# Five sixths of the modulation's matrix product computed by VectorE and ScalarE in place of TensorE

## The chip, the core and the metric

The kernel runs on one core of a Trainium2 chip. The metric is the device time of one execution in microseconds (us). TensorE (PE) multiplies matrices; loading its weights is a separate row (PEld). VectorE (DVE), ScalarE (ACT) and GpSimd (POOL) do the rest; SyncE (SP) issues nearly all DMAs, in order, from one queue.

## The reference

Two transformer blocks run one after the other. The first has two layers over 256 tokens and, in layer 0, 256 context tokens, 1024 features each. What the change touches is each layer's modulation:

```python
silu_c = jax.nn.silu(c)                 # (1, 1024)
silu_cc = jax.nn.silu(c_ctx)            # (1024,)
for layer in range(DEPTH):              # DEPTH = 2
    mod = (silu_c @ w_mod[layer] + b_mod[layer])[:, None, :]
    mod_c = silu_cc @ w_mod[layer] + b_mod[layer]
    shift1, scale1, gate1, shift2, scale2, gate2 = jnp.split(mod, N_MOD, axis=-1)
    c_shift1, c_scale1, c_gate1, c_shift2, c_scale2, c_gate2 = jnp.split(mod_c, N_MOD, axis=-1)
    h_ctx = modulate(rms_norm(ctx, norm_mix[layer]), c_shift1, c_scale1)
    h = modulate(rms_norm(x, norm_mix[layer]), shift1, scale1)
    ...
    x = x + gate1 * x_mix
    x = x + gate2 * swiglu(modulate(rms_norm(x, norm_ffn[layer]), shift2, scale2),
                           w_gate_up[layer], w_down[layer])
```

`w_mod[layer]` is 1024 x 6144: 48 blocks of 128 output features, two vectors (`c`, `c_ctx`) to multiply. Around it stand the head projections, a gated long convolution ("hyena") with a small filter network, attention, a merge of both branches with sigmoid gates, and a SwiGLU. The second block (attention, memory attention, 32 experts) is not touched.

## The kernel before

Activations lie with 128 features on the partitions; a product is over all 512 tokens in layer 0 and over 256 in layer 1. Every engine runs a program written out by hand, and semaphores (`Signal`) order them.

**The weight stream.** All weights come as units of 128 x 1024 values, 512 KB, through a ring of six slots (`NS = 6`). `stream_order` (line 237) fixes the order; unit i takes slot i mod 6, and `sync_program` issues it once the user of unit i - 6 is done (`stream.spent`). The queue is in order: a unit that has to wait holds up all behind it.

**Split weights.** For nearly all weights a product is taken in three parts of a reduced type. ScalarE rounds a unit into one of three buffers (`ac_split`, line 416; `NHI = 3`), VectorE subtracts that from the unit in place (`ve_split`, line 426), and TensorE multiplies (`pe_block`, line 435): 24 matmuls a unit. The split of a unit waits until TensorE has finished the unit three before it. Steps ask for `unit + 2`, counted in the stream's order.

**The modulation.** `pe_mod_group` (line 539) multiplies four units (a group of 4 x 128 output features) by the two conditions, 8 matmuls of 512 columns; ScalarE copies the rows out (`ac_mod_group`), and TensorE turns them onto the partitions (`pe_mod_turn`, 4 small matmuls). `ve_mod_finish` adds the bias. Each layer has 12 groups. Of layer 0, groups 0 to 4 run at the start and 5 to 11 in the first seven steps of the hyena stage; of layer 1, group 0 runs ahead of layer 0's gate/up stage, 1 to 10 in its steps 1 to 10, and 11 ahead of layer 1. `pe_prepare`, `ac_prepare` and `ve_prepare` put the groups and the filter network's steps together.

**The stages of a layer**: heads, hyena (12 products), attention with the convolution, merge (`pe_merge`: per step j two gate products, one of `w_o_attn`, and four plain matmuls of `w_o_hyena`, of which one unit serves two steps), `w_out` (`pe_mix_out`, 8 products), gate/up (`pe_gate_up`: 22 steps of two units), down (`pe_down`: two halves of 11 units). In the merge, ScalarE's and VectorE's programs for step j first make splits and then the sigmoids and multiplies of the step.

Of the kernel before, what the change touches and what calls it, by code (L numbers as in the profile page):

```python
# [232 lines left out]
STREAM = [("w_mod", 48), ("w_in", 40), ("w_o_attn", 8), ("w_o_hyena", 4), ("w_out", 8), ("w_gate_up", 44), ("w_down", 22)]  # L233
STREAM2 = [("w_xk_2", 8), ("w_in_2", 22), ("w_out_2", 8), ("w_xq_2", 8), ("w_xv_2", 8), ("w_xo_2", 8)]


def stream_order():
    units = []
    for l in range(2):
        for name, n in STREAM:  # L240
            if name == "w_mod":
                units += [(name, l, u) for u in (range(20) if l == 0 else range(44, 48))]
            elif name == "w_in":
                for u in range(24):
                    units.append((name, l, u))
                    if l == 0 and 12 <= u < 19:
                        units += [("w_mod", 0, 4 * u - 28 + m) for m in range(4)]
                for j in range(8):
                    units += [("w_in", l, 24 + 2 * j), ("w_in", l, 25 + 2 * j), ("w_o_attn", l, j)]
                    if j % 2 == 0:  # L250
                        units.append(("w_o_hyena", l, j // 2))
            elif name == "w_gate_up":
                units += [("w_mod", 1, u) for u in range(4 if l == 0 else 0)]
                for u in range(n):
                    units.append((name, l, u))
                    if l == 0 and u % 2 == 1 and 3 <= u <= 21:
                        units += [("w_mod", 1, 2 * u - 2 + m) for m in range(4)]
            elif name not in ("w_o_attn", "w_o_hyena"):
                units += [(name, l, u) for u in range(n)]
    for name, n in STREAM2:  # L260
        units += [(name, 0, u) for u in range(n)]
    return units
# [10 lines left out]
def two_blocks_kernel(nc, T):  # L273
    ctx = ExitStack()
    with ctx:
# [38 lines left out]
        rst = [sb(f"rst{i}", 512) for i in range(2)]  # L314
        PP = [sb(f"PP{i}", 512) for i in range(2)]
# [66 lines left out]
        landed = {n: (sem("d_" + n), 16) for n in ("vec", "x", "con", "fil0", "fw0", "fil1", "fw1", "mem", "wr", "br", "late",  # L382
# [74 lines left out]
        def unit(name, l, b):  # L457
            return where[name, l, b // UB]

# [79 lines left out]
        def pe_mod_group(pe, l, g):  # L539
            if g == 0:  # L540
                banks.hold((ve_mod, ("added", l, 1)), "mods", l)
            out = banks.take((ac_mod, ("rows", l, g)), "mod", l, g)
            pe.wait_ge(*banks.emptied("mod", l, g))
            pe.wait_ge(*ve_mod.at("silu", 1))
            for k in range(8):
                w, u = stream.block("w_mod", l, 32 * g + 4 * k, 4)
# [4 lines left out]
                stream.spent[u] = (pe_mod, ("group", l, g))  # L551
            ins.then_inc(*pe_mod.up("group", l, g))
            if g > 0 and g != 4:
                pe_mod_turn(pe, l, g - 1)
            if g == 3:
                pe_mod_turn(pe, l, g)

        def pe_mod_turn(pe, l, g):
            if g == 0:
                pe.wait_ge(*banks.emptied("mods", l))  # L560
                pe.wait_ge(*landed["con"])
            if g == 4:
                pe.wait_ge(*ve_mod.at("added", l, 0))
            pe.wait_ge(*ac_mod.at("rows", l, g))
            for n in range(4):
                j = 4 * g + n
                ins = pe.eng.matmul(banks.ap("mods", l)[:, 2 * j:2 * j + 2], rmod[g % 2][:, n * P:(n + 1) * P], cc("sel", 0, 2),
                                    start=True, stop=True)
            ins.then_inc(*pe_mod.up("turn", l, g))
            if g == 11:  # L570
                banks.give("mods", l)

        def ac_mod_group(ac, l, g):
            for u in range(4):
                ac_split(ac, where["w_mod", l, 4 * g + u] + 2)
            ac.wait_ge(*pe_mod.at("group", l, g))
            if g >= 2:
                ac.wait_ge(*pe_mod.at("turn", l, g - 2))
            ac.eng.activation(rmod[g % 2][:, :], banks.ap("mod", l, g), ACT.Copy).then_inc(*ac_mod.up("rows", l, g))

        def ve_mod_group(ve, l, g):
            for u in range(4):
                ve_split(ve, where["w_mod", l, 4 * g + u] + 2)
            if g == 3:
                ve_mod_finish(ve, l, 0)

        def ve_mod_finish(ve, l, part):
            j0, j1 = ((0, 16), (16, 48))[part]
            md, at = MODS[l], 8 + 24 * part
            ve.wait_ge(*pe_mod.at("turn", l, (3, 11)[part]))  # L590
            ve.wait_ge(*landed["vec"])
            ve.eng.tensor_tensor(md[:, j0:j1, :], banks.ap("mods", l)[:, 2 * j0:2 * j1].rearrange("p (j s) -> p j s", s=2),
                                 vv(("b_mod", l), j0, j1 - j0).unsqueeze(2).to_broadcast([P, j1 - j0, 2]),
                                 ALU.add).then_inc(*ve_mod.up("added", l, part))
            ve.wait_ge(*ve_mod.last())
            for s in range(2):
                ve.eng.scalar_tensor_tensor(A12S[l][:, part, :, s], md[:, at:at + 8, s], 1.0,
# [1762 lines left out]
```

## Time and profile before

| | us |
|---|---|
| median of three runs | 2406.33 |
| lowest, highest | 2399.57, 2409.31 |
| the profiled execution's own time | 2409.14 |
| its span in the profile | 2407.4 |

The profiler's page gives each engine's busy time, the queues, the chain of work that ended last and the costliest groups of instructions. Behind it, the trace can be asked for the chain in order of time (each piece with its start, its length and what it was), for a timeline of one engine (each row: start, length, engine, line, operation, output<-inputs; in brackets the engine's idle time before it and what ended that), and for the busy times in a stretch. L12 is line 12 of the kernel. SPq is SyncE's queue. Busy times of different engines overlap.

### The profile page before, as it was taken

How to read it: one execution, taken by the hardware profiler on the slowest of the kernel's cores; microseconds unless marked ns; L12 is line 12 of the kernel's file. 1: busy time of each engine (PE TensorE's matmuls, PEld its weight loads, DVE VectorE, ACT ScalarE, POOL GpSimd, SP SyncE). 2: the span in 40 equal slices, each digit the busy share in tenths (PEclk: the TensorE clock that was granted, in tenths of full speed). 3: DMA queues.
4: the chain of work that ended last, by engine and by line, in shares of the span. 5: the costliest groups of instructions: out<-in, count | busy, mean ns of one | idle time of the engine just before them, and what ended most of it. 6: DMA issues, size and time to landing. Idle time of an engine off the chain costs nothing.

```text
span 2407.4 us, 34019 instructions
## 1 busy us (share of the span) xinstructions
PE 2143.4 (89%) x14596; PEld 1636.3 (68%) x14596; DVE 1032.3 (43%) x1691; ACT 714.3 (30%) x1177; POOL 15.4 (1%) x31
## 2 busy tenths in 40 slices
PE   6989989997999999978998999986689898888886
PEld 2756667775777877668698999885488754445442
DVE  3663663334332334468655566685643311101111
ACT  3222333223322233343444445432533200000000
POOL 0000000000000000000000000000000000000000
PEclk9989999998999999988999999998799899999998
DMA  7226102132454222223145455441042799999993
GB/s 305 71 96 245 44 1 88 62 139 87 175 210 175 97 95 89 96 81 113 36 149 184 158 173 169 150 135 67 14 136 70 291 421 420 420 420 420 420 420 152
DMA packets 90495, 426.93 MB, mean 177 GB/s; under 512 B 10851, under 2 KB 12388, under 8 KB 65380
## 3 DMA queue, kind: packets, MB, share of 16 engines
q1 hardware_dynamic: 89908, 420.96, 46.2%
q10 hardware_dynamic: 432, 3.74, 0.4%
q8 instruction: 117, 1.92, 0.3%
q14 instruction: 38, 0.31, 0.0%
HBM read 423.61 MB, written 1.05 MB: 176 GB/s over the span
## 4 chain that ended last, share of the span: by engine, by line
PE 68%; DMA 12%; DVE 12%; ACT 4%; issue 3%; SPq 1%; POOL 0%; DVEq 0%; ACTq 0%; POOLq 0%
PE bank L452 42%; PE bank L1290 7%; DMA area<-in_w 6%; PE bank L1894 4%; DMA ring<-in_w 4%; PE bank L470 3%; DVE ring_r L431 2%; PE bank L1860 2%; DVE rst L500 2%; PE bank L1002 1%; PE bank L977 1%; PE bank L549 1%; ACT his_r L423 1%; DMA ring<-in_w_mod 1%; SPq L2219 1%
## 5 line engine op out<-in xcount | busy, mean ns | idle before, releaser
L452 PE MATMUL bank<-HH_r,his_r 128*128 128x256 f32 (+1 forms) x1696 | 579.9, 342 | 67.5 <-DVE ring_r L431 50.5
L452 PE MATMUL bank<-HH_r,ring_r 128*128 128x256 f32 (+1 forms) x1696 | 560.1, 330 | 0.0
L431 DVE TENSOR_TENSOR ring_r<-ring,his_r 128x1024 fp32r<-128x1024 f32 x306 | 373.1, 1224 | 412.7 <-ACT his_r L423 412.1
L452 PE MATMUL bank<-H_r,his_r 128*128 128x256 f32 (+1 forms) x1504 | 505.1, 336 | 0.0
L423 ACT ACTIVATE his_r<-ring 128x1024 fp32r<-128x1024 f32 x306 | 322.2, 1056 | 568.3 <-PE bank L452 332.2
L452 PEld LDWEIGHTS bank<-HH_r,his_r 128*128 128x128 f32 x1696 | 328.5, 194 | 111.5 <-issue 67.7
L452 PEld LDWEIGHTS bank<-HH_r,ring_r 128*128 128x128 f32 x1696 | 327.5, 193 | 29.6
L452 PEld LDWEIGHTS bank<-H_r,his_r 128*128 128x128 f32 x1504 | 292.0, 194 | 31.2 <-issue 2.6
L1876 DVE TENSOR_TENSOR tmp<-tmp,bank 128x128 f32<-128x128 f32 x64 | 18.4, 288 | 371.3 <-ACT tmp L1869 290.8
L1290 PE MATMUL bank<-VT_r,his_r 128*128 128x512 f32 (+1 forms) x352 | 120.4, 342 | 8.3 <-DVE YF_r L1103 7.8
L452 PE MATMUL bank<-area_r,his_r 128*128 128x256 f32 (+1 forms) x384 | 122.4, 319 | 0.0
L1894 PE MATMUL bank<-area,tmp 128*32 128x512 f32 x248 | 111.5, 594 | 10.7 <-DVE tmp L1915 6.7
L1290 PE MATMUL bank<-VT_r,ring_r 128*128 128x512 f32 (+1 forms) x352 | 118.4, 336 | 0.0
L1290 PE MATMUL bank<-YF_r,his_r 128*128 128x512 f32 (+1 forms) x352 | 118.4, 336 | 0.0
L470 PE MATMUL bank<-tmp,ones 128*128 128x256 f32 (+1 forms) x220 | 85.3, 494 | 32.1 <-ACT tmp L478 12.3
L1860 PE MATMUL bank<-area,KF 128*32 128x128 f32 x2144 | 89.3, 284 | 15.8 <-DMA area<-in_w 15.3
L500 DVE RECIPROCAL rst<-rst 128x256 f32<-128x256 f32 (+1 forms) x33 | 81.7, 2477 | 43.1 <-ACT rst L494 43.1
L1869 ACT ACTIVATE tmp<-bank 128x128 f32<-128x128 f32 x32 | 8.9, 278 | 299.9 <-PE bank L1860 299.9
L1860 PEld LDWEIGHTS bank<-area,KF 128*32 128x32 f32 x2144 | 72.3, 113 | 28.7 <-DMA area<-in_w 19.4
L1894 PEld LDWEIGHTS bank<-area,tmp 128*32 128x32 f32 x248 | 25.6, 110 | 85.8 <-issue 65.7
L1290 PEld LDWEIGHTS bank<-VT_r,his_r 128*128 128x128 f32 x352 | 66.4, 189 | 18.6 <-issue 4.7
L470 PEld LDWEIGHTS bank<-tmp,ones 128*128 128x128 f32 x220 | 37.7, 201 | 59.4 <-ACT tmp L478 28.8
(306 smaller groups left out, 3001.2 us busy)
## 6 DMA issues: line engine op xcount, KB each, us to landing
area<-in_w SPq DMA_DIRECT2D x98, 1024.0 KB, 27.0
ring<-in_w_in SPq DMA_DIRECT2D x102, 512.0 KB, 3.5
ring<-in_w_mod SPq DMA_DIRECT2D x96, 512.0 KB, 5.3
ring<-in_w_gate_up SPq DMA_DIRECT2D x88, 512.0 KB, 3.5
ring<-in_w SPq DMA_DIRECT2D x39, 1024.0 KB, 26.9
HH<-in_w SPq DMA_DIRECT2D x28, 1024.0 KB, 26.5
ring<-in_w_down SPq DMA_DIRECT2D x44, 512.0 KB, 3.5
con<-in_w SPq DMA_DIRECT2D x14, 1024.0 KB, 25.4
```

The source lines that it names most:

```text
L423: ac.eng.activation(hi_slot(n), stream.slot(u), ACT.Copy).then_inc(*ac_hi.up(n))
L431: ve.eng.tensor_tensor(lo_slot(u), stream.slot(u), hi_slot(n).bitcast(F32), ALU.subtract).then_inc(*ve_lo.up(n))
L452: ins = pe.eng.matmul(out, a, b, start=k == 0 and m == 0, stop=end)
L470: pe.eng.matmul(banks.ap("sum", site)[:, 0:cols], ones[:, :], s[:, 0:cols], start=n == 0, stop=n == total - 1).then_inc(*pe_sums.up(site, n))
L500: ve.eng.reciprocal(r, r).then_inc(*ve_norm.up("rstd", site))
L549: ins = pe.eng.matmul(out[32 * c:32 * c + 32, :], sc2[:, k, :], w, start=k < 4, stop=k >= 4, tile_position=(0, 32 * c))
L977: ins = pe.eng.matmul(out[:, 256 * m:256 * m + c.nkey], q[:, qb * P:(qb + 1) * P], k, start=x == 0, stop=x == len(pairs) - 1)
L1002: ins = pe.eng.matmul(out[:, 0:256], vs(kc), c.pts[g % 2][:, kc * 256:(kc + 1) * 256], start=kc == 0, stop=kc == c.nk - 1)
L1290: ins = pe.eng.matmul(out[n][:, 0:t], w, x, start=k == 0 and m == 0, stop=k == 21 and m == 2)
L1860: ins = pe.eng.matmul(out[32 * n:32 * n + 32, 0:P], HG[g % 2][:, k, 32 * j:32 * j + 32], w, start=k == 0, stop=k == 7, tile_position=(0, 3 ...
L1894: ins = pe.eng.matmul(out[32 * j:32 * j + 32, :], AT[i][:, 32 * k:32 * k + 32], w, start=k == 0, stop=k == 3, tile_position=(0, 32 * j))
L2219: sp.eng.dma_start(experts.slot(i), T[name][e, u]).then_inc(experts.arrived(i)[0], 16)
```

## The change

Only the first 16 of layer 0's 48 blocks stay on TensorE (groups 0 to 3, at the start). The other 80 blocks, 32 of layer 0 and 48 of layer 1, are each one new unit of the stream, `w_mod_rows`: 128 output features on the partitions, 1024 inputs in a row. For each, called a column below, VectorE multiplies the unit by silu(c), broadcast over the partitions, into one buffer (`rsts_flat`), and by silu(c_ctx) in place; ScalarE runs a copy over each product whose accumulator gives the row's sum, straight into `MODS`. The broadcast vectors are loaded and made in the merge stage of layer 0 (`ac_conditions`, `ac_silu`, `ve_silu`), in the attention's buffers `PT` and `PP`.

In the stream a column stands behind each weight unit of layer 0's merge (steps 1 to 7, not behind `w_o_hyena`), the first three `w_out` units, all 44 gate/up units and the first 12 down units. Splits now ask for two split units on (`two_on`), not two stream units on. The filter network's steps stay where they were; `pe_prepare` and its fellows become `pe_filter_step`.

```diff
+MOD_ORDER = [(0, j) for j in range(16, 48)] + [(1, j) for j in range(48)]
 def stream_order():
-    units = []
+    mods = iter([("w_mod_rows", l, j) for l, j in MOD_ORDER])
+    units = [("w_mod", 0, u) for u in range(16)]
     for l in range(2):
...
+        def also(wanted):
+            return [u for u in (next(mods, None) for _ in range(1 if wanted else 0)) if u]
+
+        units += [("w_in", l, u) for u in range(24)]
+        for j in range(8):
+            for name, u in (("w_in", 24 + 2 * j), ("w_in", 25 + 2 * j), ("w_o_attn", j)):
+                units += [(name, l, u)] + also(l == 0 and j)
+            if j % 2 == 0:
+                units.append(("w_o_hyena", l, j // 2))
+        for u in range(8):
+            units += [("w_out", l, u)] + also(l == 0 and u < 3)
+        for name, n in (("w_gate_up", 44), ("w_down", 22)):
+            for u in range(n):
+                units += [(name, l, u)] + also(l == 0)
...
+        def two_on(i):
+            return cut_units[min(nth[i] + 2, len(cut_units) - 1)] if i in nth else i + 2
...
+        COND = [PT[:, :], PPS[:, :]]
+
+        def ac_conditions(ac):
+            ac.wait_ge(*pe_turned.at("ctx0", 7, 0))
+            ac.wait_ge(*pe_values.at("ctx0", 7, 0))
+            for s in range(2):
+                ac.eng.dma_start(COND[s], T["conditions"][s:s + 1, :].to_broadcast([P, 1024])).then_inc(*landed[f"cond{s}"])
+
+        def ac_silu(ac):
+            for s in range(2):
+                ac.wait_ge(*landed[f"cond{s}"])
+                if s:
+                    ac.wait_ge(*ve_mod.at("condition", 0))
+                ac.eng.activation(rsts_flat[:, :], COND[s], ACT.Sigmoid).then_inc(*ac_mod.up("sigmoid", s))
+
+        def ve_mod_column(ve, n):
+            l, j = MOD_ORDER[n]
+            u = where["w_mod_rows", l, j]
+            w = stream.slot(u)
+            ve.wait_ge(*stream.arrived(u))
+            if n:
+                ve.wait_ge(*ac_mod.at("sum", n - 1, 0))
+            else:
+                ve.wait_ge(*ve_mod.at("condition", 1))
+            ve.eng.tensor_tensor(rsts_flat[:, :], w, COND[0], ALU.mult).then_inc(*ve_mod.up("product", n, 0))
+            ve.eng.tensor_tensor(w, w, COND[1], ALU.mult).then_inc(*ve_mod.up("product", n, 1))
+
+        def ac_mod_column(ac, n):
+            l, j = MOD_ORDER[n]
+            u = where["w_mod_rows", l, j]
+            for s, prod in enumerate((rsts_flat[:, :], stream.slot(u))):
+                ac.wait_ge(*ve_mod.at("product", n, s))
+                ac.eng.activation(prod, prod, ACT.Copy, accum_out=MODS[l][:, j, s:s + 1]).then_inc(*ac_mod.up("sum", n, s))
+            stream.spent[u] = (ac_mod, ("sum", n, 1))
...
         def hyena_steps(l, j):
-            return [5 + j] if l == 0 and j < 8 else [12] if l == 1 and j == 0 else []
+            return [5 + j] if l == 0 else []
...
             for j in range(8):
                 for u in merge_units(l, j):
-                    ac_split(ac, u + 2)
+                    ac_split(ac, two_on(u))
+                    ac_mod_after(ac, *stream.units[u])
+                if l == 0 and j == 0:
+                    ac_silu(ac)
                 ac.wait_ge(*(ve_out.at("merged", l, j - 1) if j else ve_cut.at("att", l, 7)))
...
             for j in range(22):
-                ac_split(ac, unit("w_gate_up", l, 16 * j) + 2)
-                ac_split(ac, unit("w_gate_up", l, 16 * j + 8) + 2)
+                for s in range(2):
+                    ac_split(ac, two_on(unit("w_gate_up", l, 16 * j + 8 * s)))
+                    ac_mod_after(ac, "w_gate_up", l, 2 * j + s)
                 ac.wait_ge(*pe_products.at("gate", l, j))
                 ac.eng.activation(AFF[:, j, 0:t], banks.ap("gate", l, j)[:, 0:t], ACT.Sigmoid).then_inc(*ac_out.up("gate", l, j))
-                if l == 0 and 1 <= j <= 10:
-                    ac_prepare(ac, 1, j)
+                if l == 0:
+                    ac_filter_step(ac, 1, j)
...
-                    ac_split(ac, unit("w_down", l, 88 * half + 4 * k) + 2)
+                    ac_split(ac, two_on(unit("w_down", l, 88 * half + 4 * k)))
+                    if k % 2 == 0:
+                        ac_mod_after(ac, "w_down", l, 11 * half + k // 2)
...
-    arrays["w_mod"] = fours(I["w_mod"])
+    arrays["w_mod"] = fours(I["w_mod"][0:1, :, 0:2048])
+    arrays["w_mod_rows"] = np.ascontiguousarray(I["w_mod"].transpose(0, 2, 1)).reshape(2, 48, P, 1024)
+    arrays["conditions"] = np.concatenate([I["c"].reshape(1, 1024), I["c_ctx"].reshape(1, 1024)], axis=0)
```

VectorE's programs change in the same places, with `ve_mod_after` behind each `ve_split`. The bias is added in pieces (`ve_mod_columns_done`), each ahead of its first use.

How the order moves, first on SP's queue in layer 0's merge. `in_w_in` are the gate weights, two a step; `pe_products` is TensorE's signal that a product is done, `ac_mod` ScalarE's that a column is summed. Before, from `w_o_attn` of step 1 to the gate weights of step 4:

```order
L2200 DMA ring<-in_w_o_attn 128x1024 [waits pe_products]
L2200 DMA ring<-in_w_in 128x1024 [waits pe_products] x2
L2200 DMA ring<-in_w_o_attn 128x1024 [waits pe_products]
L2200 DMA ring<-in_w_o_hyena 128x1024
L2200 DMA ring<-in_w_in 128x1024 x2
L2200 DMA ring<-in_w_o_attn 128x1024 [waits pe_products]
L2200 DMA ring<-in_w_in 128x1024 [waits pe_products] x2
```

Now, from the second gate weight of step 2 to the first of step 4:

```order
L2270 DMA ring<-in_w_in 128x1024
L2270 DMA ring<-in_w_mod_rows 128x1024 [waits ac_mod]
L2270 DMA ring<-in_w_o_attn 128x1024
L2270 DMA ring<-in_w_mod_rows 128x1024 [waits ac_mod]
L2270 DMA ring<-in_w_o_hyena 128x1024 [waits pe_products]
L2270 DMA ring<-in_w_in 128x1024 [waits ac_mod]
L2270 DMA ring<-in_w_mod_rows 128x1024 [waits pe_products]
L2270 DMA ring<-in_w_in 128x1024 [waits ac_mod]
L2270 DMA ring<-in_w_mod_rows 128x1024 [waits pe_products]
L2270 DMA ring<-in_w_o_attn 128x1024 [waits ac_mod]
L2270 DMA ring<-in_w_mod_rows 128x1024 [waits pe_products]
L2270 DMA ring<-in_w_in 128x1024
```

A column stands behind each weight. In step 2 the columns wait for ScalarE and the weights for TensorE; behind `w_o_hyena` it is the other way round, and the last column shown takes the slot of `w_o_hyena` itself.

On ScalarE in layer 0's gate/up, two steps before (L423 is the split, L1240 the gate's sigmoid):

```order
L423 ACTIVATE his_r<-ring 128x1024 [waits pe_products,s_w2]
L423 ACTIVATE his_r<-ring 128x1024 [waits pe_products,s_w3]
L1240 ACTIVATE area<-bank 128x512
L423 ACTIVATE his_r<-ring 128x1024 [waits pe_products,s_w4]
L423 ACTIVATE his_r<-ring 128x1024 [waits pe_products,s_w5]
L1240 ACTIVATE area<-bank 128x512
```

and one step now (L422 the split, L643 the two sums of a column, L1305 the sigmoid):

```order
L422 ACTIVATE his_r<-ring 128x1024 [waits pe_products,s_w4]
L643 ACTIVATE rst,MOD<-rst 128x1024 [waits ve_mod]
L643 ACTIVATE ring,MOD<-ring 128x1024 [waits ve_mod]
L422 ACTIVATE his_r<-ring 128x1024 [waits pe_products,s_w0]
L643 ACTIVATE rst,MOD<-rst 128x1024 [waits ve_mod]
L643 ACTIVATE ring,MOD<-ring 128x1024 [waits ve_mod]
L1305 ACTIVATE area<-bank 128x512
```

Two sums, which wait for VectorE, now stand between one split and the next. VectorE in the same step before:

```order
L431 TENSOR_TENSOR ring_r<-ring,his_r 128x1024 [waits ac_hi,s_w4]
L431 TENSOR_TENSOR ring_r<-ring,his_r 128x1024 [waits ac_hi,s_w5]
L1257 TENSOR_TENSOR area<-area,bank 128x512 [waits ac_out]
L1260 TENSOR_TENSOR area<-area,bank 128x512 [waits pe_products,ve_out]
L431 TENSOR_TENSOR ring_r<-ring,his_r 128x1024 [waits ac_hi,s_w0]
```

and now (L430 the split's subtraction, L635 and L636 the column's multiplies, L1323 and L1326 the gating):

```order
L430 TENSOR_TENSOR ring_r<-ring,his_r 128x1024 [waits ac_hi,s_w2]
L635 TENSOR_TENSOR rst<-ring,PT 128x1024 [waits ac_mod,s_w5]
L636 TENSOR_TENSOR ring<-ring,PP 128x1024
L430 TENSOR_TENSOR ring_r<-ring,his_r 128x1024 [waits ac_hi,s_w4]
L635 TENSOR_TENSOR rst<-ring,PT 128x1024 [waits ac_mod,s_w1]
L636 TENSOR_TENSOR ring<-ring,PP 128x1024
L1323 TENSOR_TENSOR area<-area,bank 128x512 [waits ac_out]
L1326 TENSOR_TENSOR area<-area,bank 128x512 [waits pe_products,ve_out]
```

Each subtraction waits for ScalarE's split, and each pair of multiplies stands behind it.

## Rows read from the trace of the kernel before

**Rows 1.** The page, section 1: busy us, share of the span, instructions.
```profile
PE 2143.4 (89%) x14596; PEld 1636.3 (68%) x14596; DVE 1032.3 (43%) x1691; ACT 714.3 (30%) x1177; POOL 15.4 (1%) x31
```
**Rows 2.** Windows, gate/up of layer 0: us; PE, PEld, DVE, ACT, POOL; clock; DMA.
```profile
593.00:883.60 290.60, 285.64 (x1315) 216.66 (x1315) 98.06 (x124) 78.90 (x96) 0.62 (x1) 0.98 0.43 152
```
**Rows 3.** Chain of waits, hyena stage of layer 0: start, length, what.
```profile
159.93 6.11 PE bank L452 x21
...
169.68 5.75 PE bank L452 x24
...
178.27 3.63 PE bank L647 x8
...
199.79 3.54 PE bank L672 x8
...
223.97 8.20 DMA ring<-in_w_in
...
234.63 7.15 PE bank L452 x24
...
242.57 22.11 PE bank L452 x96
```
**Rows 4.** Chain of waits, gate/up of layer 0.
```profile
643.17 3.46 DMA ring<-in_w_gate_up
...
677.04 1.85 PE bank L549 x16
678.89 0.98 PE bank L567 x8
```
**Rows 5.** Chain of waits, hyena stage of layer 1.
```profile
1118.99 0.79 PE bank L567 x8
```
**Rows 6.** Timeline of VectorE, gate/up of layer 0.
```profile
596.23 1.23 DVE L431 TENSOR_TENSOR ring_r<-ring,his_r 128x1024 fp32r<-128x1024 f32 x1
...
619.82 1.22 DVE L431 TENSOR_TENSOR ring_r<-ring,his_r 128x1024 fp32r<-128x1024 f32 x1 [3.97 <-ACT his_r L423]
620.96 0.53 DVE L633 TENSOR_SCALAR YF<-bank,vec 64x256 f32<-64x256 f32 x1
...
623.07 0.29 DVE L615 TENSOR_SCALAR YF<-YF 64x256 f32<-64x256 f32 x1
```
**Rows 7.** Timeline of ScalarE, gate/up of layer 0.
```profile
623.39 0.42 ACT L639 ACTIVATE YF<-YF 64x256 f32<-64x256 f32 x1 [1.89 <-DVE YF L615]
623.83 1.28 ACT L1240 ACT_TABLE_LOAD   x1
...
646.66 1.06 ACT L423 ACTIVATE his_r<-ring 128x1024 fp32r<-128x1024 f32 x1 [4.54 <-DMA ring<-in_w_gate_up]
647.62 0.58 ACT L579 ACTIVATE PP<-bank 128x512 f32<-128x512 f32 x1
```
**Rows 8.** Timeline of ScalarE, attention of layer 0: an accumulator's read and the next.
```profile
274.62 0.19 ACT L1019 ACTIVATION_READ_ACCUMULATOR PP<-bank,st 128x1 f32 x1
274.71 0.59 ACT L926 ACTIVATE VT<-bank 128x512 f32<-128x512 f32 x1
```
**Rows 9.** Timeline of ScalarE, down stage of layer 0: two cuts.
```profile
890.39 1.14 ACT L1099 ACTIVATE VT_r<-area 128x512 fp32r<-128x512 f32 x2
```
**Rows 10.** Timeline of SP's queue, merge of layer 0: end of steps 1 and 3.
```profile
401.56 0.33 SPq L2200 DMA_DIRECT2D ring<-in_w_o_attn  x1
...
441.41 0.33 SPq L2200 DMA_DIRECT2D ring<-in_w_o_attn  x1
```
**Rows 11.** Timeline of SP's queue, merge of layer 1.
```profile
1227.67 0.33 SPq L2200 DMA_DIRECT2D ring<-in_w_o_attn  x1
...
1228.52 0.91 SPq L2200 DMA_DIRECT2D ring<-in_w_in  x2
```
**Rows 12.** Timeline of ScalarE, merge of layer 1: the splits behind that burst.
```profile
1231.95 1.06 ACT L423 ACTIVATE his_r<-ring 128x1024 fp32r<-128x1024 f32 x1 [6.86 <-DMA ring<-in_w_o_attn]
1234.96 1.06 ACT L423 ACTIVATE his_r<-ring 128x1024 fp32r<-128x1024 f32 x1 [1.95 <-DMA ring<-in_w_in]
```
**Rows 13.** The page, section 6: KB each, us from issue to landing.
```profile
ring<-in_w_gate_up SPq DMA_DIRECT2D x88, 512.0 KB, 3.5
```

More of the change, by code:

```diff
@@ L550, in pe_mod_group @@
                                     tile_position=(0, 32 * c))
[L551 to L554, printed above, removed]
+                stream.spent[u] = (pe_mod, ("group", g))
+            ins.then_inc(*pe_mod.up("group", g))
+            if g > 0:
+                pe_mod_turn(pe, g - 1)
             if g == 3:
-                pe_mod_turn(pe, l, g)
-        def pe_mod_turn(pe, l, g):
+                pe_mod_turn(pe, g)
+                banks.give("mods")
@@ L568, in pe_mod_turn, with ac_mod_group @@
                                     start=True, stop=True)
[L569 to L573, printed above, removed]
+            ins.then_inc(*pe_mod.up("turn", g))
+        def ac_mod_group(ac, g):
             for u in range(4):
-                ac_split(ac, where["w_mod", l, 4 * g + u] + 2)
-            ac.wait_ge(*pe_mod.at("group", l, g))
+                ac_split(ac, where["w_mod", 0, 4 * g + u] + 2)
+            ac.wait_ge(*pe_mod.at("group", g))
@@ L605, in sin_reduced, with after, ac_mod_after, ve_mod_after @@
+        def after(name, l, u):
+            i = where[name, l, u] + 1
+            return MOD_ORDER.index(stream.units[i][1:]) if i < len(stream.units) and stream.units[i][0] == "w_mod_rows" else None
+        def ac_mod_after(ac, name, l, u):
+            n = after(name, l, u)
+            if n is not None:
+                ac_mod_column(ac, n)
+        def ve_mod_after(ve, name, l, u):
+            n = after(name, l, u)
+            if n is not None:
+                ve_mod_column(ve, n)
         def sin_reduced(ve, signal, r, k):
@@ L1164, in ve_merge @@
                 for u in merge_units(l, j):
-                    ve_split(ve, u + 2)
+                    ve_split(ve, two_on(u))
+                    ve_mod_after(ve, *stream.units[u])
+                if l == 0 and j == 0:
+                    ve_silu(ve)
                 for key, gate, w in (("oa", "ga", w0), ("oh", "gh", w1)):
@@ L1196, in ac_mix_out @@
                 if j < 8:
-                    ac_split(ac, unit("w_out", l, 8 * j) + 2)
+                    ac_split(ac, two_on(unit("w_out", l, 8 * j)))
+                    ac_mod_after(ac, "w_out", l, j)
                 if j:
@@ L1205, in ve_mix_out @@
             t = tokens(l)
-            ve.wait_ge(*modulated(l, 1))
+            if l == 0:
+                ve_mod_columns_done(ve, 0, 16, 24)
+            ve.wait_ge(*ve_mod.at("added", l, 16))
             for j in range(8):
-                ve_split(ve, unit("w_out", l, 8 * j) + 2)
+                ve_split(ve, two_on(unit("w_out", l, 8 * j)))
+                ve_mod_after(ve, "w_out", l, j)
+                if l == 0 and j == 4:
+                    ve_mod_columns_done(ve, 0, 24, 40)
+                    ve_mod_scale(ve, 0, 1)
                 ve.wait_ge(*pe_products.at("mix", l, j))
@@ L1252, in ve_gate_up @@
             for j in range(22):
-                ve_split(ve, unit("w_gate_up", l, 16 * j) + 2)
-                ve_split(ve, unit("w_gate_up", l, 16 * j + 8) + 2)
+                for s in range(2):
+                    ve_split(ve, two_on(unit("w_gate_up", l, 16 * j + 8 * s)))
+                    ve_mod_after(ve, "w_gate_up", l, 2 * j + s)
                 o = AFF[:, j, 0:t]
@@ L1327, in ve_down @@
                         ve_cut_tile(ve, VTR[:, m % 4, 0:t], YFR[:, m % 4, 0:t], AFF[:, m, 0:t], ("ff", l, half, m))
-                    ve_split(ve, unit("w_down", l, 88 * half + 4 * k) + 2)
+                    ve_split(ve, two_on(unit("w_down", l, 88 * half + 4 * k)))
+                    if k % 2 == 0:
+                        ve_mod_after(ve, "w_down", l, 11 * half + k // 2)
+                if l == 0 and half == 0:
+                    ve_mod_columns_done(ve, 0, 40, 48)
+                if l == 0 and half == 1:
+                    for j0, j1 in ((0, 16), (16, 24), (24, 40), (40, 48)):
+                        ve_mod_columns_done(ve, 1, j0, j1)
+                    for part in range(2):
+                        ve_mod_scale(ve, 1, part)
+                ve.wait_ge(*ve_mod.at("added", l, 40))
                 for n in range(4):
@@ L1591, in ac_residual @@
                 if j < 8:
-                    ac_split(ac, unit(name, 0, 8 * j) + 2)
+                    ac_split(ac, two_on(unit(name, 0, 8 * j)))
                 if j:
```

183 lines of the change are left out of this document (77 added, 106 removed).

## The prediction, made before the changed kernel was run

> **What bounds the kernel now.** I read the page first for shares: TensorE is busy 89% of the span, VectorE 43%, ScalarE 30% [rows 1]. Averages say little here, so next come the stages of layer 0, where all the moved work goes: over the gate/up stage TensorE is busy 285.6 of 290.6 us, VectorE 98.1, ScalarE 78.9 [rows 2]. Then the chain of waits: in layer 0 it is almost all TensorE products of 24 matmuls, 5.5 us each, with the modulation groups between them [rows 3, 4]. What else holds TensorE is a weight unit that is late: landed, rounded by ScalarE, subtracted by VectorE. So two questions decide: what TensorE loses in work, and whether units still come at one per 5.5 us.
>
> **Removed: TensorE's groups.** One group is 1.85 us of products and 0.98 us of turning, 2.83 us on the path [rows 4]. In layer 0's hyena stage there are seven. From 169.68 to 264.68 us (95.0 us) eleven products run; alone they need 11 x 5.53 = 60.8 (the last four take 22.11), and the filter 3.63 + 2 x 3.54 = 10.7. The rest, 23.5 us, is groups, a late unit behind four modulation units (8.20 us of waiting) and splits that stood behind the convolution of their own step; such a gap of 3.6 us also stands just before 169.68 [rows 3]. With `two_on` splits run two weight units ahead, so both go: **-27.1 us**. Layer 1's turn, 0.79 us, goes [rows 5]: **-0.8**. Group 4 of layer 0 and groups 0 and 11 of layer 1 ran while TensorE waited for a norm; I give them nothing (2.83 us each at most).
>
> **Added: one column.** It is two VectorE multiplies and two ScalarE sums of 128x1024. The nearest rows are the split's halves, same size: on VectorE 1.22 us, with the next operation starting 1.14 us after its start [rows 6]; on ScalarE 1.06, the next after 0.96 [rows 7]. What a sum adds is the read of its accumulator; the next operation starts 0.09 us after that read does [rows 8]. I take 1.07 us a sum. 80 columns are 187 us of VectorE and 171 of ScalarE. That fits the idle time, but the engines wait for each other. Per weight unit: ScalarE split 1.06, hop 0.10, VectorE split 1.14, first multiply 1.22, hop 0.05, two sums 2.14: **5.7, with the second multiply's end 5.8 us**. ScalarE takes the next split only behind its sums, so nothing in this ring overlaps. It is longer than TensorE's 5.5.
>
> At nothing I cost the two loads of the conditions, their two sigmoids and two multiplies: they stand in the merge's step 0, which has no column, under 19.9 us of TensorE's work (some 6 us if that cover were gone). The biases move in number, not on the path.
>
> **Gate/up of layer 0** (from 593.03 to the down stage's first matmul at 883.59 us). A step is two units, 11.6 us, and its gating: sigmoid 0.60, hop, two multiplies at 0.61, against the 1.16 of the next split, so 0.7 more: 12.3 us where TensorE has 11.0. The filter of layer 1 hangs on the same engines: in three steps six small VectorE operations (620.96 to 623.36) and a sine, 4.0 us with what they shut out, and a table load of 1.28, so 5.3 each [rows 6, 7]; the taps' eight operations 6.4; two pairs of copies 2.0: 24.3 in all. The stage's first split ends 3.9 us in (597.46 [rows 6], less 0.5 for the group's copy ahead of it), so the last, of unit 43, ends at 3.9 + 20 x 12.3 + 5.8 + 24.3 = 280.0 us. Before the down stage can begin, three columns (3.4 us each), two gatings (1.9), two more splits (1.1 and 2.3) and a cut (1.3) are still owed: 18.7 us, of which TensorE works 5.5. That gives 298.7 against 290.6: **+8.1 us**. The ten groups there are worth 28.3 us, and a late unit 5 more [rows 4]; the new ring takes these back. If the ring is 5.5 or less, the stage ends near 265 us (22 x 11.0 + 10.7, and some fill); if a landing comes into it, at 6.4 a unit, near 325.
>
> **Down of layer 0.** A unit has two cuts each on top. ScalarE: 1.10 for the cuts, split 1.06, hop, VectorE 1.14 + 1.22, hop, sums 2.14: 6.8 us against 5.5 [rows 9]. Twelve units carry a column: 12 x 1.3 = **+16 us** (0 if the ring is short, 23 if landings join it).
>
> **The merge stage: who frees a slot.** The SP queue has six slots and issues in order. A slot of a weight is free when TensorE is done, one of a column when ScalarE has summed it. Before, `w_o_hyena` serves two steps, and the unit that takes its slot is the third in line (the `w_o_attn` issued at 401.56 us, at the end of the odd step), with 11 us of work ahead of its use; pairs of steps last 39.85 us [rows 10]. Now the slot goes to the column behind `w_o_attn` of the odd step, and the next gate weight is queued behind that. Layer 1 shows what follows: of a burst issued from 1227.67 [rows 11] the first lands by 1231.95, the third by 1234.96 [rows 12], so the second, my estimate between them, after 5.6 us. With two splits TensorE starts 8.1 us late. It does not end there: `w_o_hyena` makes the count of units odd, so gate weights then take the slots of columns. By the two rows of a pair, from the end of an odd step:
> - first gate unit 8.1 to 15.1 (1.5 us more than 5.5, a cold start as in the 7.15 us of 234.63 [rows 3]), second to 20.6;
> - `w_o_attn`'s split stands behind two columns, two sigmoids and the merging multiplies: 21.5 to 27.0, hyena to 30.4;
> - third gate unit: issued when the column before is summed, 24.9; lands after 3.5 us [rows 13]; 30.9 to 36.4;
> - fourth: issued behind the next column, 34.3; 40.3 to 45.8. `w_o_attn` likewise: issued at 43.7, 49.7 to 55.2, hyena to 58.6.
>
> So 58.6 + 0.3 instead of 39.85: 19.0 us a pair, three pairs: **+57 us**. A fourth wait stands before `w_out`: the last merged tile comes only behind two columns, so the first product ends 21.8 us after the merge and not 5.5: +16.3. The first square stands on ScalarE behind a column, and TensorE's sum waits 5.4 for it: **+21.7** in all. Bounds for merge and `w_out` together: 0, if units and columns happen to be early, and 110, if every landing in the pair takes the 7.3 us of the third in the burst.
> The Trainium skill, "DMA: Bandwidth & Descriptors", on how a DMA triggers, gives a fixed 2.0 us and bytes over 436 GB/s: 3.2 us for a unit alone, 4.4 as second. By it, an estimate, four waits would be 1.2 us shorter each and six single landings 0.3, about 7 us less in the sum; the burst's landings [rows 12] are the slower ones, so the sum keeps them.
>
> **Sum:** -27.1 - 0.8 + 8.1 + 16 + 57 + 21.7 = +74.9 us. On the profiled execution's 2409.1 that is 2484.0; it stands 2.8 above the median of the three runs, so the forecast is **2481 us**.
>
> **Rivals.**
> - *Room on the engines* (faster): the waits between the two engines are filled and slots come early everywhere. Gain: 27.1 + 0.8 + 28.3 + 5 = 61, time 2345. For it: 57% of VectorE's and 70% of ScalarE's time is idle [rows 1]. Against it: one buffer of products, six slots, one order. It decides at a ring of 5.5 us and at an issue of the gate weight 8 us before use. The Trainium skill, "Perfetto Trace Analysis", section on the most-contended engine, says to find the bottleneck by occupancy and improve that engine first. By that rule this rival would hold.
> - *Only the merge stalls*: the ring stays under 5.5, so gate/up gains 25.6 and down loses nothing: -27.9 - 25.6 + 78.7 = +25.2, time 2432. For it: the ring is only 0.3 us over.
> - *Landings join the ring*: a column and the next weight are issued together when an old column is summed; at 5.6 us they are just in time, at 6.4 gate/up costs 26 more and down 7: 2514.
> - *The odd slots don't matter*: only the four waits cost, 8.1 each, 32 in place of 78.7: 2435.
>
> **Chances.** Forecast 0.50, landings join 0.15, only the merge 0.12, slots harmless 0.12, room 0.08, and 0.03 near no change. About 0.5% is what a measurement of this kernel can tell from none. Faster 0.08, same 0.03, slower 0.89. The range leaves out room and the worst landings: 2425 to 2525.
>
> **What would show it.** In the merge, TensorE idle four times some 8 us for a gate weight or `w_out`, released by a landing; SP's queue waiting for ScalarE's sums; pairs of 59 us. In gate/up, steps of 12 to 13 us, TensorE's idle released by VectorE's split in each unit, and some 13 us before the down stage; its units at 6.8 us for twelve. Hyena of layer 0 with steps of 5.5. Wrong: if sums or multiplies take under 0.9 us, if the idle of TensorE in the merge is under 20 us, or if its gaps in gate/up lie only at the filter's steps.

## The result, and the profile after

The changed kernel takes **2498.85 us** (median of four runs, 2496.66 to 2501.24) against 2407.28 us of the kernel before on the same chip: ratio 1.039, 95% interval 1.036 to 1.041, so 91.6 us slower. The profiled execution's span is 2495.8 us, 88.4 more than before.

The page of the changed kernel, section 1, then section 4 (the chain that ended last) and the column's two operations from section 5 (busy, mean ns | idle before):

```profile
PE 2128.2 (85%) x14116; PEld 1627.3 (65%) x14116; DVE 1218.1 (49%) x1857; ACT 881.0 (35%) x1479; POOL 19.1 (1%) x31
...
PE 47%; DVE 18%; DMA 15%; ACT 10%; issue 8%; SPq 1%; POOL 0%; DVEq 0%; ACTq 0%; POOLq 0%
...
L643 ACT ACTIVATE rst<-rst 128x1024 f32<-128x1024 f32 x80 | 84.9, 1061 | 213.2 <-DVE rst L635 213.2
...
L635 DVE TENSOR_TENSOR rst<-ring,PT 128x1024 f32<-128x1024 f32 x80 | 97.5, 1219 | 0.0
```

TensorE has 480 matmuls less, those of 20 groups, and is busy 15 us less [rows 1], while the program is 88 us longer. The last line of section 5 has the multiply at the 1.22 us that I took.

Where the 88.4 us lie, from landmarks in both traces (sums in layer 0's merge; the reciprocal of each norm; the first matmul of a stage), with what the prediction had:

| stretch | before | after | difference | predicted |
|---|---|---|---|---|
| start to the first merged tile of layer 0 | 382.4 | 355.8 | -26.6 | -27.1 |
| merge and `w_out`, to the norm's reciprocal | 191.3 | 276.4 | +85.1 | +78.7 |
| norm and gate/up, to the first down matmul | 309.8 | 311.9 | +2.1 | +8.1 |
| down, to the next reciprocal | 134.5 | 175.5 | +41.0 | +16 |
| layer 1 and all behind it | 1389.3 | 1376.1 | -13.2 | -0.8 |

**Hyena of layer 0.** The chain of waits of the changed kernel (start, length, what):

```profile
159.27 12.94 PE bank L451 x48
172.21 3.63 PE bank L707 x8
175.84 11.20 PE bank L451 x48
187.04 3.43 PE bank L732 x8
190.48 5.51 PE bank L451 x24
...
199.42 38.48 PE bank L451 x168
```

Nothing but products of 5.5 us and the filter's three pieces is left; groups and late units [rows 3] are gone.

**Merge.** SP's queue around the end of an odd step (start, length, what it issues):

```profile
374.97 0.33 SPq L2270 DMA_DIRECT2D ring<-in_w_mod_rows  x1
375.34 0.43 SPq L2270 DMA_DIRECT2D ring<-in_w_in  x1
...
399.52 0.33 SPq L2270 DMA_DIRECT2D ring<-in_w_in  x1
...
409.38 0.33 SPq L2270 DMA_DIRECT2D ring<-in_w_in  x1
...
419.01 0.33 SPq L2270 DMA_DIRECT2D ring<-in_w_o_attn  x1
...
435.83 0.33 SPq L2270 DMA_DIRECT2D ring<-in_w_mod_rows  x1
```

From 374.97 to 435.83 is a pair of steps: 60.9 us; the next two take 59.3 and 59.4, where they took 39.85 [rows 10]. TensorE's first matmuls behind each wait (in brackets the idle time and who ended it):

```profile
382.74 0.76 PE L451 MATMUL bank<-HH_r,his_r 128*128 128x512 f32 x1 [7.80 <-DVE ring_r L430]
...
415.68 0.56 PE L451 MATMUL bank<-HH_r,his_r 128*128 128x512 f32 x1 [3.88 <-DVE ring_r L430]
...
562.48 0.77 PE L451 MATMUL bank<-VT_r,his_r 128*128 128x512 f32 x1 [7.93 <-DVE ring_r L430]
...
574.70 0.79 PE L451 MATMUL bank<-YF_r,his_r 128*128 128x512 f32 x1 [6.16 <-DVE area_r L1152]
```

The first is the weight behind the burst, the second the fourth gate weight of the pair, the third the weight behind the burst ahead of `w_out`, the last the merged tile that came behind two columns. The other two bursts cost 7.65 us (at 443.45) and 7.92 (at 503.04): four idle times of some 8 us, as forecast.

**Gate/up.** One step in the chain of waits, from a column's multiply to the one two units on:

```profile
875.78 1.23 DVE rst L635
877.04 1.15 ACT rst L643 x2
...
881.17 1.22 DVE ring_r L430
...
888.04 1.23 DVE rst L635
```

12.26 us a step. In this stretch the chain has no TensorE product and no landing: only VectorE and ScalarE hand work to and fro.

**Down.** One round in the chain of waits, in which TensorE multiplies two units (24 matmuls each), and its first matmul behind it:

```profile
962.91 8.54 PE bank L1356 x24
...
971.47 3.61 DMA ring<-in_w_down
...
975.10 1.07 ACT his_r L422
...
977.41 1.23 DVE rst L635
...
978.66 1.15 ACT rst L643 x2
...
980.94 0.53 ACT VT_r L1148
...
981.49 0.70 DVE YF_r L1152
...
982.24 0.79 PE L1356 MATMUL bank<-VT_r,his_r 128*128 128x512 f32 x1 [5.31 <-DVE YF_r L1152]
```

Not two engines go round here but four stations: TensorE finishes unit u and frees its slot, the unit three on lands in it, ScalarE rounds that unit (two ahead of its use), sums a column, and only then makes the cut that TensorE needs for its next matmuls. TensorE, which had the second unit to work on meanwhile, then stands idle for 5.3 us: 19.3 us for two units (962.91 to 982.24), where 11.0 are work.

### The profile page after: what moved, and what is told of

Same layout as the page of the kernel before. It is cut to its first block, busy times and chain, and to the rows that moved or that the text cites. A ratio compares the mean times of both kernels' runs of the same rounds, so it can differ in the third digit from the quotient of the medians.

```text
span 2495.8 us, 33607 instructions
## 1 busy us (share of the span) xinstructions
PE 2128.2 (85%) x14116; PEld 1627.3 (65%) x14116; DVE 1218.1 (49%) x1857; ACT 881.0 (35%) x1479; POOL 19.1 (1%) x31
## 4 chain that ended last, share of the span: by engine, by line
PE 47%; DVE 18%; DMA 15%; ACT 10%; issue 8%; SPq 1%; POOL 0%; DVEq 0%; ACTq 0%; POOLq 0%
PE bank L451 25%; DMA area<-in_w 6%; PE bank L1356 5%; DMA ring<-in_w 5%; PE bank L1972 4%; DVE ring_r L430 3%; DVE rst L635 3%; ACT rst L643 3%; ACT his_r L422 3%; DVE rst L502 3%; PE bank L472 3%; PE bank L1938 2%; DMA ring<-in_w_in 2%; PE bank L1026 1%; PE bank L1051 1%
## 5 line engine op out<-in xcount | busy, mean ns | idle before, releaser
L430 DVE TENSOR_TENSOR ring_r<-ring,his_r 128x1024 fp32r<-128x1024 f32 x306 | 373.1, 1224 | 439.4 <-ACT his_r L422 439.1
L422 ACT ACTIVATE his_r<-ring 128x1024 fp32r<-128x1024 f32 x306 | 321.3, 1054 | 377.3 <-PE bank L451 174.0
L643 ACT ACTIVATE rst<-rst 128x1024 f32<-128x1024 f32 x80 | 84.9, 1061 | 213.2 <-DVE rst L635 213.2
L635 DVE TENSOR_TENSOR rst<-ring,PT 128x1024 f32<-128x1024 f32 x80 | 97.5, 1219 | 0.0
L636 DVE TENSOR_TENSOR ring<-ring,PP 128x1024 f32<-128x1024 f32 x80 | 97.5, 1219 | 0.0
```

What stands on the lines that cost most here:

```text
L422: ac.eng.activation(hi_slot(n), stream.slot(u), ACT.Copy).then_inc(*ac_hi.up(n))
L430: ve.eng.tensor_tensor(lo_slot(u), stream.slot(u), hi_slot(n).bitcast(F32), ALU.subtract).then_inc(*ve_lo.up(n))
L635: ve.eng.tensor_tensor(rsts_flat[:, :], w, COND[0], ALU.mult).then_inc(*ve_mod.up("product", n, 0))
L636: ve.eng.tensor_tensor(w, w, COND[1], ALU.mult).then_inc(*ve_mod.up("product", n, 1))
L643: ac.eng.activation(prod, prod, ACT.Copy, accum_out=MODS[l][:, j, s:s + 1]).then_inc(*ac_mod.up("sum", n, s))
```

## The experiments

Three causes were to be told apart: the ring of two engines (5.7 us against 5.5), the six slots that columns share with weights, and how far ahead the splits run. In each table row below, "pair" is two merge steps, from one odd step's merged tile to the next (the last of three where one value stands), "merge" runs from the first merged tile to the norm's reciprocal and so has `w_out` in it; gate/up and down as above.

**1. Columns left out by stage.** A flag in `stream_order` keeps a column's place and drops its unit:

```diff
-                units += [(name, l, u)] + also(l == 0)
+                units += [(name, l, u)] + also(l == 0, name == "w_gate_up")
```

> Left out: the twelve columns of the down stage (their MODS entries hold the bias alone). Theory 'a column's landing is in the ring of the down stage': the stage, from its first product to the rstd of mix1, was 134.5 us before and 175.5 after; without its columns it falls to 132 to 135, the granted clock there goes back to 1.0, and the whole to 2457 us (2498.9 less 41). Rival 'the splits run ahead (two_on) and the cuts stand behind them, columns or not': the stage stays over 150 us and the whole over 2470. My own prediction had priced the twelve at 16 us, which would give 2483.

> Left out: the 21 columns of the merge and the 3 of w_out. Theory 'columns in the six slots stall the gate weights': pairs of merge steps go from 59.4 back to 39.9 us (-60), merge end to rstd from 77.7 to 53 (-25), the whole to 2414 us. Rival 'two_on puts the splits behind the sigmoids and merging multiplies, and that costs by itself': pairs stay over 44 us and the whole over 2430. Gate/up and down keep 312 and 175 us in both.

> Left out: all 80 columns. What is left is the gain of taking the groups off TensorE and of two_on. Theory 'nothing else costs': merge pairs 39.9, w_out 53, norm and gate/up 284 us (22 steps of 11.0 and 10.7 of filter behind 23 to 32 of norm and start), down 132 to 134, the whole 2340 us (2336 to 2350). Rival 'part of the loss is in two_on or the new loads': the whole over 2365, with the excess in merge or down. So the columns would cost 158 us in all, of which 60 + 25 in merge and w_out, 28 in gate/up, 41 in down.

| | pair | merge | gate/up | down | whole |
|---|---|---|---|---|---|
| changed | 59.4 | 276.4 | 311.9 | 175.5 | 2498.9 |
| no_down | 59.6 | 275.8 | 312.1 | 136.0 | (3857) |
| no_merge_out | 39.9 | 191.3 | 312.4 | 174.3 | 2411.8 |
| none | 39.9 | 191.3 | 269.2 | 134.1 | (3724) |

The two totals in brackets can't be compared: without all the modulations the experts' stage took another course. The windows of `none` have 10333 matmuls behind 1900 us, in 1824 us; the page of the changed kernel has 14116 in the whole. The stages ahead of it stand as measured. They put the price of the columns at 85.1 us in merge and `w_out`, 42.7 in gate/up and 41.4 in down. What the removal (with `two_on`) gains in gate/up is 40.6 us (309.8 to 269.2), more than the 33 that I had; the expectation of 284 us for this stage was too high. The rival that `two_on` costs by itself falls in all three: what it costs together with the columns is the subject of experiment 5.

**2. One sum.** The second condition's multiply and sum are left out.

```diff
-            ve.eng.tensor_tensor(w, w, COND[1], ALU.mult).then_inc(*ve_mod.up("product", n, 1))
...
-            for s, prod in enumerate((rsts_flat[:, :], stream.slot(u))):
+            for s, prod in enumerate((rsts_flat[:, :],)):
```

> Left out: the second condition's product and sum in every column (one multiply and one sum each stay). Theory 'gate/up is 0.3 us a unit over TensorE, a ring through two engines': the ring falls from 5.8 to 4.7 us (split 1.06, hop, split 1.14, multiply 1.22, hop, sum 1.06), so steps go from 12.25 to 11.0 us and the stage from 312 to 285. Merge and down are set by landings, so they lose only what the sum took: pairs 59.4 to 54 to 57, down 175 to 150 to 163 us; the whole 2498.9 - 27 - 10 - 18 - 3 = about 2440. Rival 'landings set gate/up too': the steps there stay over 11.6 us, with TensorE's waits ended by landings behind the split. Rival 'work of the engines is all that counts': merge and down fall by half of their excess, the whole to 2415.

2436.6 us. Steps of gate/up, once the filter's are past, fall from 12.2 to 11.0 us, as with no columns at all (`none`: 11.0), and the stage to 279.3 us; of the other 10 us over `none`, 7 lie ahead of the first sigmoid and 7 in the first ten steps, where the filter's work stands, and some come back at the end. Pairs fall to 54.4 and down to 168.7 us, which is more than the 150 to 163 expected. So gate/up is the ring of two engines, and 1.1 us less in it brings TensorE back; the merge and down are not. Expected for the whole was 2440.

**3. Slots of their own.** Four buffers that are idle in turn (the unused part of `area`, `KX`, `VX`, `KF`) take the columns; ScalarE's queue loads them three ahead, and the six slots hold weights alone.

```diff
+        def rows_slot(n):
+            if n < 24:
+                return area[:, 6144 + 1024 * (n % 4):7168 + 1024 * (n % 4)]
+            if n % 4 < 2:
+                return (KX, VX)[n % 4].rearrange("p k t -> p (k t)")
...
+            if n and n + 3 < len(MOD_ORDER):
+                ac_load_column(ac, n + 3)
-            for s, prod in enumerate((rsts_flat[:, :], stream.slot(u))):
+            for s, prod in enumerate((rsts_flat[:, :], rows_slot(n))):
```

> All 80 columns, in four slots of their own (idle parts of area, KX, VX, KF), loaded by ScalarE's queue three columns ahead; the six ring slots hold weights alone. Order of the work on ScalarE and VectorE as in the changed kernel. Theory 'slots stall merge and down, the ring of two engines stalls gate/up': merge pairs go to 40 to 46 us (a column is 5.7 us beside three or four units of 5.5, and the sigmoids stand behind it), w_out to 60 to 66 us (the columns still stand ahead of the squares), down units with a column from 9.4 to 6.8, the stage to 150 us; gate/up stays at steps of 12.2, 312 us. The whole about 2498.9 - 50 - 14 - 25 = 2410. Rival 'the ring of two engines is the cost in merge and down too': pairs stay over 50 and the whole over 2450. Rival 'slots are the cost everywhere': gate/up steps fall to 11.0 and the whole to 2380.

**4. The same, and sums one unit later.**

```diff
-            n = after(name, l, u)
-            if n is not None:
-                ac_mod_column(ac, n)
+            if ac.due is not None:
+                ac_mod_column(ac, ac.due)
+            ac.due = after(name, l, u)
```

> As own_slots, and ScalarE sums a column one unit later, behind the next split, so that VectorE's multiplies and ScalarE's sums overlap: per unit ScalarE 3.2 us and VectorE 3.6 (4.3 and 4.7 with a cut in down), both under TensorE's 5.5. Theory: all stages go back to TensorE: merge pairs 39.9 to 41, w_out 53 to 58, gate/up steps 11.0 and the stage 285, down 134; the whole 2340 to 2360 us, faster than before by 2 to 3%. Rival 'ScalarE and VectorE are too full for it': gate/up steps over 11.6 and the whole over 2400. Rival 'twice the traffic delays the weights': TensorE's waits in gate/up end with landings, and the whole lies at 2370 or more.

| | pairs | merge | gate/up | down | whole | to before (95%) |
|---|---|---|---|---|---|---|
| own_slots | 41.1, 40.3, 39.3 | 198.5 | 311.8 | 148.0 | 2389.2 | 0.991 (0.988 to 0.994) |
| own_lagged | 39.9 | 191.3 | 269.2 | 137.4 | 2329.7 | 0.966 (0.963 to 0.968) |

The two causes come apart. Own slots take all but 7 us of the merge's loss away and leave gate/up where it was (311.8 against 311.9); the lag takes the ring away. Both kernels came out faster than expected (2410, and 2340 to 2360). With both, the kernel is 79.6 us faster than before (2409.4 in these rounds) and 169 faster than the changed one. Windows over gate/up (length; PE, PEld, DVE, ACT, POOL busy; clock; DMA share; GB/s), of the changed kernel:

```profile
632.30:944.10 311.80, 270.25 (x1086) 207.01 (x1086) 209.85 (x222) 176.75 (x277) 5.67 (x6) 0.94 0.43 149
```

and of `own_lagged`:

```profile
548.60:817.70 269.10, 258.95 (x1087) 203.85 (x1088) 209.33 (x222) 170.18 (x273) 5.67 (x6) 0.98 0.49 170
```

VectorE does the same 209 us of work in both. `own_slots`, with the columns in the same buffers as here, also has 209.9, and takes 311.8 us: between these two only the order of VectorE's work against ScalarE's is another. ScalarE's timeline there:

```profile
705.40 1.06 ACT L439 ACTIVATE his_r<-ring 128x1024 fp32r<-128x1024 f32 x1 [1.87 <-PE bank L468]
705.42 0.34 ACTq L663 DMA_DIRECT2D area<-in_w_mod_rows  x1
706.36 1.05 ACT L671 ACTIVATE rst<-rst 128x1024 f32<-128x1024 f32 x1
707.31 0.18 ACT L671 ACTIVATION_READ_ACCUMULATOR rst<-rst 128x1 f32 x1
707.40 1.04 ACT L671 ACTIVATE area<-area 128x1024 f32<-128x1024 f32 x1
```

Split and sums follow each other without a gap, and the idle time ahead of the split is ended by TensorE, no longer by VectorE. So the profile shows that the ring is broken.

**5. How far ahead the splits run.** Slots shared again, as in the changed kernel; one weight unit ahead instead of two, in down (both layers) and in layer 0's merge.

```diff
+        def one_on(i):
+            return cut_units[min(nth[i] + 1, len(cut_units) - 1)]
...
-                    ac_split(ac, two_on(unit("w_down", l, 88 * half + 4 * k)))
+                    ac_split(ac, one_on(unit("w_down", l, 88 * half + 4 * k)))
```

> The changed kernel, but in the down stage (of both layers) ScalarE and VectorE split one weight unit ahead instead of two; slots shared as before. Theory 'in the down stage the cuts for the next 256 rows stand on ScalarE behind a split that waits for a landing which TensorE's last unit has only just made possible': one unit ahead the landing has a unit more time, and only the 6.8 us of the engines' ring are left: stage 175.5 to 147 to 153 us, the whole 2470 to 2476. Rival 'a column's own landing in a shared slot is the wait': the stage stays over 168 and the whole over 2490.

> The changed kernel, but in layer 0's merge the splits run one weight unit ahead instead of two; slots shared. Theory 'SP's queue and the lead of the splits stall together': a split still waits for a weight issued at a column's sum, but one unit more in hand is worth one split, two sums and a landing: pairs 59.4 to 46 to 54 us, the whole 2455 to 2485. Rival 'the late issue alone decides', as my prediction had it: pairs stay 57 to 61 us and the whole 2490 or more.

**6. The lag in shared slots**, in gate/up and down; then with one unit ahead in all stages.

```diff
+            if name not in ("w_gate_up", "w_down") and ac.due is not None:
+                ac_mod_column(ac, ac.due)
+                ac.due = None
```

> The changed kernel, but in gate/up and down ScalarE sums a column one unit later, behind the next split; slots shared, splits two ahead. Theory 'a lag alone only moves the wait into SP's queue': a column's slot comes free 5 us later, the next column and the weight behind it are issued then and land after 4.8 us, and the split of that weight is what ScalarE does next: 1.06 + 2.2 + 4.8 = 8.1 us a unit, steps of 16 us, gate/up 312 to 370 to 395 us, down 175 to 195, the whole 2560 to 2600. Rival 'the overlap is all that was missing': gate/up 269 us, down 140, the whole 2420.

> As lag_shared, and the splits run one weight unit ahead instead of two in merge (layer 0), w_out, gate/up and down. No buffer is added. Theory: a weight issued at a late sum now has 5.5 + 2.3 = 7.8 us to land, more than 4.8: gate/up steps 11.3 us and the stage 269 to 275 us, down 137 to 150, merge as in the run with one ahead there, w_out near 77: the whole 2370 to 2420 us. Rival 'slots stay the limit': gate/up over 300 us and the whole over 2450.

| | pairs | merge | gate/up | down | whole |
|---|---|---|---|---|---|
| down_one_ahead | 59.4 to 61.1 | 277.2 | 311.9 | 147.1 | 2475.1 |
| merge_one_ahead | 50.2 to 50.9 | 242.5 | 312.0 | 175.2 | 2459.8 |
| lag_shared | 61.0 to 61.4 | 279.9 | 374.7 | 169.4 | 2555.1 |
| shared_one | 50.2 to 50.8 | 240.3 | 270.5 | 136.8 | 2393.1 |

In down one unit of lead less gives 28.4 of the 41 us back, and the stage then stands where own slots had put it (148.0): in both the 6.8 us of the engines' ring remain (980.45 to 987.22 below). The whole falls by 24 us only; layer 1 and all behind it take 4.8 us more, for one split less is made ahead of layer 1's first norm (3.7 us, below). The chain of `down_one_ahead` in down has no landing in it:

```profile
980.45 1.23 DVE rst L638
...
983.99 1.04 ACT VT_r L1151 x2
985.03 0.96 ACT his_r L422
...
987.22 1.23 DVE rst L638
```

In the merge it gives about half of what a pair had lost (9.1 of 19.5 us). SP's queue in `merge_one_ahead` still stands still once a pair, behind TensorE, and then sends a burst:

```profile
403.95 0.33 SPq L2273 DMA_DIRECT2D ring<-in_w_o_attn  x1
424.31 0.33 SPq L2273 DMA_DIRECT2D ring<-in_w_mod_rows  x1
424.68 0.43 SPq L2273 DMA_DIRECT2D ring<-in_w_in  x1
```

Between two bursts its chain is one piece of 151 matmuls, 38.67 us from 385.62. So the late issue behind the burst, as predicted, costs 10 us a pair by itself (50.3 against 39.9), and the three further waits of a pair need the lead of two as well. Whether the column behind `w_o_attn` in the odd steps, put elsewhere, would free the rest in shared slots was not tried.

The lag alone makes it worse. The chain of `lag_shared` in gate/up, one unit:

```profile
859.26 1.13 ACT rst L643 x2
860.39 1.05 ACT ring L643 x2
861.44 0.02 issue
861.46 0.33 SPq L2273
861.79 0.04 issue
861.83 4.47 DMA ring<-in_w_gate_up
```

A later sum frees the slot later, the weight is queued behind the next column, and its split is what ScalarE has to do next: steps of 16.3 us, 16 expected. Down was expected at 175 to 195 us and took 169.4, 6 less than in the changed kernel; why was not tested. With one unit of lead the same lag works (270.5 us). `shared_one` is 0.8% faster than before (ratio 0.992, 95% interval 0.989 to 0.995) with no buffer added; its merge still costs 49 us over that of `none`.

## Why the prediction was right, and where a size was off

The sign, the place and the range held: 2481 forecast, 2425 to 2525 given, 2498.85 measured. Point by point:

- *Hyena, -27.1*: measured -26.6, of which the stages themselves -27.2. The first product of layer 0 ended later at the start, since a split asked for in group 3 waited for its weight (the chain: a landing of 7.47 us from 38.87), and most of that was made good before the hyena stage, whose first matmul starts at 158.71 against 158.08.
- *Merge and `w_out`, +78.7*: measured +85.1, and 85.1 by leaving those columns out. The pair was put at 58.9 us and took 59.4 to 60.7, with luck in it: the working had 17.5 us of idle time and 1.5 of slower products a pair, and the windows over the three pairs (TensorE busy 46.8, 44.2 and 46.3 us, `none`: 39.9) have 13 to 15 us idle and 4 to 7 of slower products. It had also put the waits down to slots and order alone; `merge_one_ahead` shows that about half of them need the lead of two as well. The burst's second landing came 5.2 us after the burst began and not 5.6; in `w_out` a third unit was late as well (the chain has a landing of 3.46 us at 577.66), which the working had left out.
- *Gate/up, +8.1*: measured +2.1. The step of 12.3 us is right (12.25 in steady state) and `one_sum` and `own_lagged` show its cause to be the ring. Too small was what leaves: 40.6 us by `none`, not 33, of which 2.8 is told below.
- *Down, "Twelve units carry a column: 12 x 1.3 = +16 us"*: measured +41. **This is the term that was mis-sized.** The ring of 6.8 us is right: `own_slots` and `down_one_ahead` have it at +13.9 and +13.0 against `none`. The step left out that the cut for the next matmuls stands on ScalarE behind a split two units ahead, whose weight can only be loaded when TensorE has finished the unit it is on; so some 28 us come on top. The prediction had looked for landings in gate/up ("landings join the ring", 26 there and 7 in down); of these two stages they came in down alone, where a cut is queued behind the split.
- *Layer 1, "its turn, 0.79 us"*: measured -13.2. About 6 are these rows of the kernel before's chain, in the norm ahead of layer 1:

```profile
1028.15 0.95 ACT his_r L423
...
1029.20 1.23 DVE ring_r L431
...
1034.41 0.96 ACT his_r L423
1035.45 1.23 DVE ring_r L431
```

  With no `w_mod` units between the weights, both splits are made ahead of the norm, and from reciprocal to first product it takes 16.5 us (1119.65 to 1136.14) and not 22.4 (1018.07 to 1040.50). `down_one_ahead`, where one of the two splits is made there again, bears this out: from this reciprocal to the next took 30.5 us before, 24.5 in `none` and 28.2 in that run. The same is worth 2.8 us ahead of gate/up in `none`. Some 3 more come by layer 1's merge and 3 to 4 behind it; what makes these was not tested.

The errors in down (+25), merge (+6.4), layer 1 (-12) and gate/up (-6) partly cancel; that the sum was only some 13 us short, and not 31, is luck. The rival "room on the engines" did not hold for the changed kernel: the engine with the largest busy share lost work and the time rose. `own_lagged` lands at 2329.7 where that rival said 2345; the room was there, and order and slots kept it shut. The Trainium skill ("Perfetto Trace Analysis", section "Identifying the Most-Contended Engine") says which engine to improve first, TensorE here by its 89%; the changed kernel shows that this alone does not make a move of its work pay, and `own_lagged` that it can.

## What to carry to other kernels

Work that leaves a full engine for two half-empty ones pays only if the two need not wait for each other inside one period: add up the whole round (here 5.7 us against 5.5) and, where it is longer, let one side run an item behind. Before a new kind of transfer joins an in-order queue with shared slots, write down who frees each slot and what stands behind that on the freeing engine; a lead can be too long (a split two units ahead cost 28 us more in down than one unit ahead), and the lag that saves 43 us with free slots costs 63 without.

## What the runs showed of the hardware

- A wait was paid for twice, by the clock. Over the merge, windows of the changed kernel and of `none`:

```profile
355.80:573.40 217.60, 162.49 (x575) 118.14 (x573) 90.58 (x92) 79.27 (x126) 0.00 (x0) 0.88 0.31 110
```

```profile
354.90:494.30 139.40, 139.40 (x561) 105.23 (x560) 43.38 (x49) 31.64 (x41) 0.00 (x0) 1.00 0.22 80
```

  TensorE is busy 162.5 us at a granted clock of 0.88 and 139.4 at 1.00 (2.4 GHz), but the first window also holds 14 matmuls more of `w_out`. Up to the first matmul of `w_out` (562.48 and 493.0) the products are the same and take 156.4 against 138.1 us: 18 of the 68 us lost by then are slower products, not idle time. In gate/up it is 270.3 against 258.9, in down 143.3 against 130.5. So TensorE's busy time fell by 15 us only, though 20 groups of 2.8 us had left it. The prediction had 1.5 us a pair for a cold start.
- Landings of 512 KB in the merge's chain: alone (`w_o_attn`) 3.4 to 3.6 us; with a column's load issued 0.4 us behind, 3.7 to 4.0; the second of a burst 4.7 to 5.0 us after its own issue, 5.1 to 5.3 after the burst began; the weight behind a column in `lag_shared` mostly 4.3 to 5.4, at most 6.1. The Trainium skill, "DMA: Bandwidth & Descriptors", section "Anatomy of one DMA — SWDGE (gpsimd) path", has a fit of 2.0 us and bytes over 436 GB/s for DMAs issued from GpSimd; the estimate from it, 3.2 us alone and 4.4 as second, is short of both for these, which SyncE issues.
- With 170 GB/s in layer 0's gate/up of `own_lagged`, twice the 86 of `none`, the median landing of a gate/up unit there was 4.2 us against 3.4, and TensorE lost nothing by it: both stages last 269 us.
- A DMA issued from ScalarE's queue (0.34 us at 705.42, above) ran beside ScalarE's split; the next activation started 0.96 us after the split had, as elsewhere.
- A copy of 128x1024 with a sum on ScalarE: the next operation starts 1.04 to 1.14 us after it, read of the accumulator included; the prediction had 1.07.
